# Recurrent-mixer stage of a three-block forward pass: key transposes, one table of exponentials and a head's vector work stand in another order

## The reference, cut to what matters

```python
def _forget(z, lb):
    f = lb + (1 - lb) * jax.nn.sigmoid(z.astype(jnp.float32))
    return _heads(jnp.log(f)), _heads(1 - f)          # log gate, key

def step(state, inp):                                  # one chunk of tokens
    qc, kc, vc, gc = inp
    bcum = jnp.cumsum(gc, axis=-2)
    b_ref = bcum[..., mid:mid + 1, :]
    b_end = bcum[..., -1:, :]
    inter = jnp.einsum('bhck,bhkv->bhcv', qc * jnp.exp(bcum), state)
    scores = jnp.einsum('bhtk,bhsk->bhts', qc * jnp.exp(bcum - b_ref), kc * jnp.exp(b_ref - bcum))
    intra = jnp.einsum('bhts,bhsv->bhtv', jnp.where(mask, scores, 0.0), vc)
    new_state = (jnp.exp(b_end[..., 0, :])[..., None] * state
                 + jnp.einsum('bhsk,bhsv->bhkv', kc * jnp.exp(b_end - bcum), vc))
    return new_state, inter + intra

o = o_forward + o_backward
y = (_rmsnorm(o, norm_g) * jax.nn.silu(gate)) @ w_out  # w_out is the next stage
```

## Time and profile before

| | us |
|---|---|
| median of 3 runs | 3799.02 |
| lowest, highest | 3797.12, 3800.05 |
| the profiled execution | 3793.87 |
| its span | 3792.1 |
| span of the stage, from PE's first projection to PE's last instruction | 209.2 to 890.5 |

### The profile page before, as it was taken

The page is one execution under the profiler, slowest core; times in us unless marked ns, Lnnn a source line. Parts: engine busy times, 40 slices in busy tenths (PEclk is TensorE's granted clock), DMA queues, the critical chain, the costliest instruction groups (busy, mean ns, idle before and its releaser), DMA issues. The chain is left out here.

```text
span 3792.1 us, 57945 instructions
## 1 busy us (share of the span) xinstructions
PE 3485.8 (92%) x24707; PEld 2601.8 (69%) x24707; DVE 2033.7 (54%) x3155; ACT 1345.7 (35%) x2228; POOL 690.2 (18%) x354
## 2 busy tenths in 40 slices
PE   8999999996899988898899999999897968999998
PEld 5778778785544436656677657888576766878886
DVE  4158787774198885722244336332567575065422
ACT  3146666663211114423244323322442122233321
POOL 0000000002100000202122113443630001434442
PEclk9999999998999999999899999999898989999999
DMA  7622222223366561303121132332320002323332
GB/s 268 220 70 54 67 68 54 54 58 90 102 186 188 186 196 52 106 15 80 29 62 45 46 104 85 99 95 61 94 59 2 3 3 57 97 82 100 95 90 71
DMA packets 517590, 331.15 MB, mean 87 GB/s; under 512 B 31356, under 2 KB 493749, under 8 KB 517078
## 3 DMA queue, kind: packets, MB, share of 16 engines
q1 hardware_dynamic: 517334, 327.45, 29.7%
HBM read 316.93 MB, written 10.49 MB: 86 GB/s over the span
## 5 line engine op out<-in xcount | busy, mean ns | idle before, releaser
L3768 POOL TENSOR_TENSOR tl_wl<-tl_w,tl_wh 128x1024 fp32r<-128x1024 f32 (+1 forms) x104 | 245.9, 2365 | 679.3 <-ACT tl_wh L3881 679.1
L1383 PE MATMUL cv_bank<-hT,cv_w 128*128 128x512 f32 x768 | 343.4, 601 | 13.7 <-DMA cv_w<-in_conv_w_in_dram 13.7
L1534 DVE SCALAR_TENSOR_TENSOR conv_u<-cv_pad,vec,conv_u 128x512 f32<-128x512 f32 x480 | 319.3, 746 | 0.0
L1383 PEld LDWEIGHTS cv_bank<-hT,cv_w 128*128 128x128 f32 x768 | 143.1, 191 | 194.6 <-issue 180.0
L2568 POOL TENSOR_TENSOR mp_wl<-mp_w,mp_wh 128x1024 fp32r<-128x1024 f32 x72 | 173.5, 2412 | 318.3 <-ACT mp_wh L2642 318.3
L3881 ACT ACTIVATE tl_wh<-tl_w 128x1024 fp32r<-128x1024 f32 (+1 forms) x104 | 108.5, 1043 | 332.2 <-PE tl_bank L3805 329.7
L797 PE MATMUL hg_bank<-hg_hh,hg_wh 128*128 128x512 f32 x512 | 207.3, 405 | 4.6 <-PEq L194 4.6
L799 PE MATMUL hg_bank<-hg_hh,hg_wl 128*128 128x512 f32 x512 | 202.8, 396 | 0.0
L798 PE MATMUL hg_bank<-hg_hl,hg_wh 128*128 128x512 f32 x512 | 202.5, 395 | 0.0
L3803 PE MATMUL tl_bank<-tl_room,tl_wh 128*128 128x512 f32 x464 | 183.0, 394 | 12.0 <-POOL tl_wl L3768 11.2
L3805 PE MATMUL tl_bank<-tl_room,tl_wl 128*128 128x512 f32 x464 | 183.4, 395 | 0.0
(11 more groups left out here) (761 smaller groups left out, 8687.9 us busy)
## 6 DMA issues: line engine op xcount, KB each, us to landing
cv_ada<-in_w_ada_dram SPq DMA_DIRECT2D x48, 1024.0 KB, 7.8
hg_w<-in_hgrn_w_in_dram SPq DMA_DIRECT2D x64, 512.0 KB, 7.0
mp_w<-in_w_mlp_dram SPq DMA_DIRECT2D x64, 512.0 KB, 3.9
open_w<-in_ada_w_dram SPq DMA_DIRECT2D x12, 2048.0 KB, 10.0
cv_w<-in_conv_w_in_dram SPq DMA_DIRECT2D x48, 512.0 KB, 4.1
tl_w<-in_w_ffn_in_dram SPq DMA_DIRECT2D x44, 512.0 KB, 3.8
fr_w<-in_w_in_dram SPq DMA_DIRECT2D x26, 512.0 KB, 3.8
side_w<-in_w_in_dram SPq DMA_DIRECT2D x24, 512.0 KB, 4.0
```

The costliest lines, as they stand in the source:

```text
L1383: ins = pe.matmul(ps[n % RING][:, :], W[n % SLOTS][:, k * P:(k + 1) * P], K.hT[:, k, :], start=(k == 0), stop=(k == KD - 1))
L1534: ins = dve.scalar_tensor_tensor(o, x, by, o, ALU.mult, ALU.add)
L3768: pool.tensor_tensor(WL[u % SPLIT][:, 0:n, :], W[u % RAW][:, 0:n, :], WH[u % SPLIT][:, 0:n, :].bitcast(F32), ALU.subtract).then_inc(low, 1)
```

## The change

Only the order of instructions in this stage changes; what is computed stays.

- PE: the five key transposes leave `recur` and become `turn_keys(d, h)`. Those of direction 0 stand in the last EARLY group (ZB, context tokens) after its first step, those of direction 1 in the G group after its third. For the last head they stay where they were.
- ACT: `early` is cut into `forward_gate` (empty ZF, split Q) and `backward_gate` (empty ZB, split G). Behind `forward_gate` now come `exps(1, h-1)`, `turn(0, h-1)` and `log(0, h)`, and only then `backward_gate(h)`. `turn(1, h-1)` moves between the emptying of Q and of G. `log(1, h-1)` goes ahead of the inverse root. One ACT_TABLE_LOAD more is needed in each head.
- DVE: `finish` goes behind `sums(1)`, the low part of G behind `products(1, h-1)`, the low part of ZB of the next head behind `recur(1, h-1)`.

```diff
--- before.py
+++ after.py
@@ -783,7 +783,7 @@
                     pe.wait_ge(sq_ok, h + 1)
                     pe.matmul(SC[:, :], K.ones[:, :], osq[:, :], start=True, stop=True).then_inc(ms_ok, 1)
 
-                def project(h, groups, owed=None, square=None):
+                def project(h, groups, owed=None, square=None, keys=None):
                     for n, (m, c) in enumerate(groups):
                         g = place(h, (m, c))
                         if c == 0 and split(h, m) > 0:
@@ -799,6 +799,8 @@
                             ins = pe.matmul(bank[:, 0:w], wl[:, k, :], hi[:, k, :], start=False, stop=(k == KD - 1))
                             if owed is not None and n == 0 and k == 2:
                                 states(*owed)
+                            if keys is not None and n == len(groups) - 1 and k == (2 if len(groups) == 2 else 0):
+                                turn_keys(*keys)
                             if square is not None and n == 1 and k == 2:
                                 mean_square(square)
                         ins.then_inc(proj, 1)
@@ -838,8 +840,7 @@
                         ins = pe.matmul(SC[q:q + 64, t0:t0 + 64], lv[:, 0, a + q:a + q + 64], lv[:, 0, t0:t0 + 64], start=True, stop=True)
                     ins.then_inc(sc_ok, 1)
 
-                def recur(d, h):
-                    p = h % 2
+                def turn_keys(d, h):
                     first = 0 if d == 0 else 1
                     pe.wait_ge(prod_ok, 2 * h + (d + 1))
                     if h or d:
@@ -850,6 +851,10 @@
                     for n in range(2):
                         ins = pe.transpose(KV[:, n * P:(n + 1) * P], ks[d][:, n * P:(n + 1) * P], K.ident[:, :])
                     ins.then_inc(tr_ok, 1)
+
+                def recur(d, h):
+                    p = h % 2
+                    first = 0 if d == 0 else 1
                     if d == 1:
                         pe.wait_ge(at_ok, 2 * h + 1)
                     elif h:
@@ -879,19 +884,21 @@
                     ins.then_inc(half_ok if d == 0 else out_ok, 1)
 
                 project(0, GROUPS)
-                project(1, EARLY)
+                project(1, EARLY, keys=(0, 0))
                 recur(0, 0)
-                project(1, LATE, owed=(0, 0))
+                project(1, LATE, owed=(0, 0), keys=(1, 0))
                 recur(1, 0)
                 for h in range(2, NH):
-                    project(h, EARLY, owed=(1, h - 2), square=h - 2)
+                    project(h, EARLY, owed=(1, h - 2), square=h - 2, keys=(0, h - 1))
                     recur(0, h - 1)
-                    project(h, LATE, owed=(0, h - 1))
+                    project(h, LATE, owed=(0, h - 1), keys=(1, h - 1))
                     recur(1, h - 1)
                 states(1, NH - 2)
                 mean_square(NH - 2)
+                turn_keys(0, NH - 1)
                 recur(0, NH - 1)
                 states(0, NH - 1)
+                turn_keys(1, NH - 1)
                 recur(1, NH - 1)
                 states(1, NH - 1)
                 mean_square(NH - 1)
@@ -957,10 +964,12 @@
                     act.wait_ge(ln_ok, h + 1)
                     act.activation(ors[:, :], ors[:, :], ACT.Exp, scale=-0.5).then_inc(rs_ok, 1)
 
-                def early(h):
+                def forward_gate(h):
                     evacuate(h, ZF, 0)
                     evacuate(h, ZF, 1)
                     weights_high(Q, h, done(h, ZF, 1))
+
+                def backward_gate(h):
                     evacuate(h, ZB, 0)
                     evacuate(h, ZB, 1)
                     weights_high(G, h, done(h, ZB, 1))
@@ -969,12 +978,15 @@
                     evacuate(h, Q, 0)
                     if h + 1 < NH:
                         weights_high(ZF, h + 1, done(h, Q, 0))
+                    if h:
+                        turn(1, h - 1)
                     evacuate(h, G, 0)
                     if h + 1 < NH:
                         weights_high(ZB, h + 1, done(h, G, 0))
                     act.preload_act_table_set(LOG_EXP_SET)
 
-                early(0)
+                forward_gate(0)
+                backward_gate(0)
                 act.preload_act_table_set(LOG_EXP_SET)
                 log(0, 0)
                 late(0)
@@ -982,19 +994,22 @@
                 for h in range(1, NH + 1):
                     if h >= 2:
                         square(h - 2)
+                    log(1, h - 1)
+                    if h >= 2:
                         inverse_root(h - 2)
-                    log(1, h - 1)
                     if h < NH:
-                        early(h)
+                        forward_gate(h)
                         act.preload_act_table_set(LOG_EXP_SET)
-                    turn(0, h - 1)
-                    exps(1, h - 1)
-                    if h < NH:
+                        exps(1, h - 1)
+                        turn(0, h - 1)
                         log(0, h)
+                        backward_gate(h)
                         late(h)
-                    turn(1, h - 1)
-                    if h < NH:
                         exps(0, h)
+                    else:
+                        turn(0, h - 1)
+                        exps(1, h - 1)
+                        turn(1, h - 1)
                 square(NH - 1)
                 inverse_root(NH - 1)
 
@@ -1105,21 +1120,22 @@
                 for h in range(1, NH):
                     products(0, h - 1)
                     gates(1, h - 1)
+                    sums(1, h - 1)
                     if h >= 2:
                         finish(h - 2)
-                    sums(1, h - 1)
                     weights_low(Q, h)
-                    weights_low(G, h)
                     gates(0, h)
                     recur(0, h - 1)
                     products(1, h - 1)
+                    weights_low(G, h)
                     sums(0, h)
                     if h + 1 < NH:
                         weights_low(ZF, h + 1)
-                        weights_low(ZB, h + 1)
                     else:
                         gates(1, h)
                     recur(1, h - 1)
+                    if h + 1 < NH:
+                        weights_low(ZB, h + 1)
                 products(0, NH - 1)
                 sums(1, NH - 1)
                 finish(NH - 2)
```

## The result

The changed kernel takes 3805.40 us (median of 17 runs, 3801.49 to 3811.15), the kernel before 3796.84 us in 17 runs beside it: ratio 1.0022, 95% interval 1.0014 to 1.0029, or 8.4 us more (5 to 11). The sum of the prediction was +5.7. The profiled executions have spans of 3800.9 and 3792.1 us.

The account below looks back on a forecast made before the run. PE was taken to bound the kernel, with 6 us idle in 80. The terms -41.1 + 32.0 + 5.6 + 4.0 + 5.2 = +5.7 us on the 3799.0 us median gave 3804.7 us; 8-in-10 range 3795 to 3813.

Parts of the forecast that it names:

- Key waits gone: At the first key-value product, 28 waits of 1.47 us for ACT's key copy go: -41.1 us.
- G waits for its low weights: PE's G group waits 2.13 us for its low weights in each of 15 heads: +32.0 us.
- L869, now L874: PE waits 0.4 us for the addition of both masked scores in 14 heads: +5.6 us.
- Breaks: Transposes and restarts break PE's stream of matmuls 44 times, 0.09 us each: +4.0 us.
- First head: First key-value product starts 3.6 us later, behind the exponentials, and 1.6 us is lost to the clock: together 5.2 us.
- Clock in the middle: PE's clock in the middle of the stage stays 1.00, so no time is lost there.
- rival 2: PE's clock falls behind the 2.1 us gap in every head, 1.6 us lost 15 times: +30, 3829 us; 6%.
- the range of 41.0 to 42.0: The prediction is wrong if a head's period leaves these bounds in us; 41.2 to 41.6 us was expected.
- The table-load rule: A table load on ACT costs 1.28 us; the skill page's added 1.38 us drain would mean 21 us more.
- ACT as the next bound: ACT and DVE need 31.1 us from G's start to the key copy, PE 31.6; ACT 1 us slower brings waits back.

Follow-up runs that it names:

- e9: PE's program of the changed kernel with the whole ACT and DVE programs of the kernel before: 3835.69 us, ratio 1.0097.
- e1: The kernel before with key transposes inside the projections and ACT's key copies moved to match, DVE in its old order: 3794.14 us, ratio 0.9992.
- e3: The changed kernel with backward_gate ahead of log(0, h) on ACT, for one table load more: 3783.92 us, ratio 0.9967.
- e6: The changed kernel with a further table load right ahead of the split of G, for h of 1 and more: 3844.76 us, ratio 1.0126.
- e4: The changed kernel with the first head's forward key copy right behind forward_gate, ahead of the exponentials: 3799.84 us, ratio 1.0007.
- e12: e5 with the inverse root again ahead of log(1, h-1), on ACT only: 3774.05 us, ratio 0.9940.
- e10: The kernel before with DVE's four moves of the change and nothing else: 3837.52 us, ratio 1.0110.
- e5: The changed kernel with backward_gate ahead of log(0, h) on ACT and G's low part ahead of products(1) on DVE: 3767.38 us, ratio 0.9916.
- e8: e5 with the first head's key copy right behind forward_gate: 3765.30 us, ratio 0.9915.
- e2: The changed kernel with ACT's old order except the moved key copies, and DVE keeping two of its four moves: 3777.8 us, ratio 0.9950.
- e7: e2 with the backward key transposes three steps later in the G group: 3778.05 us, ratio 0.9945.
- e11: e2 with log(1) ahead of the root on ACT and sums(1) ahead of finish on DVE: 3775.22 us, ratio 0.9945.

## Why the prediction was right

The mechanism and the places were right; this is its sum, term by term, against the profile. That 3804.7 came within 1 us of 3805.40 is partly luck: the forecast stood on a median of 3 runs that was 2.2 us too high (3799.02 for 3796.84), and its rise of 5.7 was too low by 2.7 to 2.9 (8.4 by the ratio, 8.6 by the medians).

- *Key waits gone, -41.1.* Right: the 28 are gone. That it is worth anything hangs on the order of the other engines: e9 has the waits longer, e1 has them in L874.
- *G waits for its low weights, +32.0.* 30.0: 2.00 us in 15 heads for 2.13. PE reached G at T + 6.71 and not T + 6.56. e3 confirms the link to `states`, e6 prices one link more.
- *L869, now L874, +5.6.* 0.31 a head, 4.3 for the same 14 heads.
- *Breaks, +4.0.* P fell by 0.24: -2.94 + 2.00 + 0.31 leaves 0.39 a head for breaks and all else, against the 0.27 of the sum, so some 5.5 us.
- *First head, 3.6 + 1.6.* The key copy made L867 start at 264.36 and not 259.53, 4.8 us later; 1.3 of this comes from the start-up of the stage, ahead of all that was changed: the last slow matmul (0.63 us) there starts at 214.36 us and not at 211.46. In the other twelve profiled kernels, whose PE program is the same up to there, it starts between 211.80 and 214.49, in no order of the changes. So 3.6 was right to 0.1. The clock was mis-sized: 264.4 to 268.0 us ran at 0.50, the 1.2 GHz level throughout, and that held up `states` and the log behind it (T + 4.73 in this head, not T + 3.33). The rest of the Q group's lateness, 5.84 - 4.83 = 1.0 us, and of the first period, 42.73 - 41.32 = 1.4, make 2.4 us.
- *Clock in the middle, 0.* Wrong: 2 of 14 periods lost 1.57 us each, 3.1 in all. The forecast held rival 2 for a case of all heads or none; it came in some, in 4 of 14 periods in e4 and in 13 of 14 in e6. By it two periods of the changed kernel left the range of 41.0 to 42.0 that the prediction gave. The evidence for 0 was thin as well: the stretch of clock 1.00 behind the gap of 2.2 us holds 1.13 us of PE work and ends 1.8 us behind the gap. In the changed kernel the slow matmuls begin at 484.79, 1.5 us behind the gap's end, so that stretch could hardly have shown a fall:

```profile
484.79 0.63 PE L797 MATMUL hg_bank<-hg_hh,hg_wh 128*128 128x512 f32 x1
```

The last head took 2.4 us more from its Q group to its last output transposes (898.87 - 849.57 against 889.41 - 842.54), of which 2.00 are the fifteenth G wait; the sum had 2.13 for it. Together: start-up 1.3, first head 3.6 + 2.4, the 14 periods -3.4 + 3.1, last head 2.4: 9.4 us at the stage's end, 8.8 in the span. Of these 1.3 is chance, as far as the traces tell. By size the errors of the sum half cancel: the G wait and L874 came 3.3 us lower than forecast, the breaks, the first head's clock and the clock in the middle 5.4 higher.

*The table-load rule.* e6 puts a load by itself into the chain, and the wait grew by 51.3 / 15 - 2.00 = 1.42 us; of P's 2.96, 1.57 is the clock, and 1.39 is left for the load and its hand-over. The load's own 1.28 fills most of it; in the changed kernel the split also began 0.11 us ahead of the sigmoids' end (480.87 against 480.11 + 0.87), while in e6 it starts 0.02 us behind the load. The page "ScalarE: Activation LUTs" of the Trainium skill ("What ACT_TABLE_LOAD costs") has 2.66 us for a switch, load and drain. The trace disagrees, in the rows too: 478.81 + 1.28 = 480.09, and the sigmoid starts at 480.11.

*ACT as the next bound.* "The copy is ready 0.5 us early" and "PE stays the bound, by little" held with the margin named. In the changed kernel the copy ends at 515.40 + 0.37 = 515.77 and PE's product starts at 516.27:

```profile
515.40 0.37 ACT L955 ACTIVATE hg_kT<-hg_bank 128x256 f32<-128x256 f32 x1
```

```profile
516.27 0.94 PE L867 MATMUL hg_bank<-hg_v,hg_kT 128*128 128x128 f32 x6
```

In e12 ACT's order makes the log later, and L867 waits at once.

What the forecast did not see is that PE's part and DVE's part of the change are a loss each when run alone (e9 +1.0%, e10 +1.1%) and that the whole is +0.2%; ACT's part was not run alone. Nor did it see that two exchanges more turn the +0.2% into -0.8% (e5, e8).

## What to carry to other kernels

A wait of an engine that is the bound is worth its length only if the next-latest input of the same group has slack: follow each releaser back before a wait is counted as won, the split of the next weights included. When a period stays the same to 0.01 us while the wait moves from one line to another (e2, e7, e11), the line that waits doesn't set it; look for a ring through the other engines, and in it for an instruction that could stand ahead of its neighbour. An instruction that two engines need soon (here the split of the next weights) belongs ahead of one that must wait for a third, even at the price of a table load (e3: 1.1 us a head won with one load of 1.28 us more).

## What was not expected of the hardware

A gap of PE of the same length did not always cost clock. Behind G's gap of 2.00 us the granted clock fell in 2 of 15 heads of the changed kernel and in 4 of 15 of e4; behind 3.42 us in e6 in 14 of 15, all but the first; in e10 it fell behind the first two gaps of 2.51 us, and the 13 after them, beside others of 1.5 in the same head, left it at 1.00:

```profile
280.00:320.00 40.00, 35.06 (x271) 29.87 (x272) 30.59 (x56) 23.13 (x43) 0.00 (x0) 0.96 0.24 63
...
360.00:880.00 520.00, 457.14 (x4765) 389.24 (x4766) 389.49 (x692) 299.39 (x522) 0.00 (x0) 1.00 0.20 55
```

So the length of one gap does not decide it alone; what else does stays open. One fall cost about 1.6 us: 42.88 - 41.32 in the changed kernel, 42.92 - 41.32 in e4, 44.28 - 41.32 - 1.42 in e6. The Trainium skill ("TensorE: Matmul & The Clock Gate", Part 1: The HAM clock gate) says that the gate judges activity in windows that run free of the program; by that rule equal gaps could fall well or badly. The scatter is in line with it, but no run here shows the windows themselves.
